# A one-core transformer block on Trainium2: the first weight unit cast in halves, two Gelus moved ahead of an exponential, an earlier residual, and a last root on ScalarE

## The reference

```
xn = rmsnorm(h, norm1_g);  p = xn @ w_in                     # 43 units of 128 columns
h  = h + mixer(p)                                            # attention, RWKV-7 recurrence, gates, w_proj, w_out
xn = rmsnorm(h, norm2_g);  q = xn @ peer_wq                  # 16 units
s  = q . subkeys;          top 16 of 128, twice; top 16 of the 256 sums   # per token and head
gates = softmax(best_s)
out[c] = sum over picked experts of  gelu(peer_u[e] . xn[c]) * gate[c, e] * peer_v[e]
return rmsnorm(h + out, normf_g)
```

## Time and profile before

| | |
|---|---|
| median of 3 runs | 1052.23 (1051.84 to 1052.33) |
| the profiled execution, its time | 1051.79 |
| its span in the trace | 1050.0 |
| TensorE busy | 1038.8 of the span |
| VectorE, ScalarE, GpSimd busy | 703.3, 640.2, 474.1 |
| granted TensorE clock, mean | 0.999 |
| data read from HBM | 179.37 MB, 172 GB/s over the span |

### The profile page before, as it was taken

How to read it: one execution, slowest core, us unless ns; L and a number is a source line. 1 busy time by engine, 2 the same in 40 slices (tenths; PEclk the granted TensorE clock), 3 DMA queues, 4 the chain that set the end, 5 groups by cost and what they waited for, 6 DMA issues and landing times.

```text
span 1050.0 us, 22101 instructions
## 1 busy us (share of the span) xinstructions
PE 1038.8 (99%) x6992; PEld 915.7 (87%) x6992; DVE 703.3 (67%) x1625; ACT 640.2 (61%) x1251; POOL 474.1 (45%) x228
## 2 busy tenths in 40 slices
PE   9999999999999999999999999999999999999997
PEld 8998899999998888888888888878888888888886
DVE  7765555445459999697888888855555555555554
ACT  7773475555566555657888888864544544544544
POOL 4685533884269888887777777730000000000000
PEclk9999999999999999999999999999999999999999
DMA  7463312556545555555444444455555555555554
GB/s 263 159 217 107 121 44 81 181 183 219 180 141 184 194 181 191 169 183 177 160 157 153 155 156 157 160 165 196 194 188 197 192 190 197 192 189 199 189 191 140
DMA packets 52136, 181.03 MB, mean 172 GB/s; under 512 B 5812, under 2 KB 7860, under 8 KB 51965
## 3 DMA queue, kind: packets, MB, share of 16 engines
q1 hardware_dynamic: 51660, 179.91, 51.2%
q10 hardware_dynamic: 432, 0.55, 0.2%
HBM read 179.37 MB, written 1.06 MB: 172 GB/s over the span
## 4 chain that ended last, share of the span: by engine, by line
PE 89%; DVE 9%; ACT 1%; DMA 0%; issue 0%; ACTq 0%; DVEq 0%
PE PS L436 19%; PE PS L888 11%; PE PS L889 11%; PE PS L887 11%; PE PS L440 10%; PE PS L426 6%; PE PS L427 5%; PE PS L428 5%; PE PS L838 2%; PE PS L839 1%; DVE PS L1429 1%; DVE PS L1808 1%; DVE PS L1812 1%; DVE con L1815 1%; PE PS L590 1%; DVE arena L1778 1%
## 5 line engine op out<-in xcount | busy, mean ns | idle before, releaser
L1324 POOL TENSOR_TENSOR lo<-raw,hi 128x1024 fp32r<-128x1024 f32 x191 | 463.4, 2432 | 191.8 <-ACT hi L934 179.7
L934 ACT CAST hi<-raw 128x1024 fp32r<-128x1024 f32 x331 | 346.5, 1047 | 193.0 <-DMA raw<-in_v_units 170.9
L436 PE MATMUL PS<-xb,hi 128*128 128x512 f32 x1088 | 279.3, 398 | 1.0 <-ACT arena L1209 1.0
L1383 DVE TENSOR_TENSOR lo<-raw,hi 128x1024 fp32r<-128x1024 f32 x140 | 171.6, 1226 | 157.4 <-ACT hi L934 157.4
L436 PEld LDWEIGHTS PS<-xb,hi 128*128 128x128 f32 x1088 | 194.9, 189 | 38.1 <-issue 2.4
L887 PE MATMUL PS<-hi,xb 128*128 128x512 f32 x512 | 199.3, 389 | 0.0
L889 PE MATMUL PS<-lo,xb 128*128 128x512 f32 x512 | 199.2, 389 | 0.0
L888 PE MATMUL PS<-hi,xb 128*128 128x512 f32 x512 | 199.2, 389 | 0.0
L440 PEld LDWEIGHTS PS<-xb,lo 128*128 128x128 f32 x1088 | 148.4, 190 | 11.0
L440 PE MATMUL PS<-xb,lo 128*128 128x256 f32 x1088 | 151.4, 282 | 0.0
L887 PEld LDWEIGHTS PS<-hi,xb 128*128 128x128 f32 x512 | 96.1, 188 | 20.1
(11 more groups left out here) (309 smaller groups left out, 1455.1 us busy)
## 6 DMA issues: line engine op xcount, KB each, us to landing
raw<-in_u_units SPq DMA_DIRECT2D x128, 512.0 KB, 3.3
raw<-in_v_units SPq DMA_DIRECT2D x128, 512.0 KB, 3.2
raw<-in_w_in_units SPq DMA_DIRECT2D x43, 512.0 KB, 3.3
raw<-in_w_q_units SPq DMA_DIRECT2D x16, 512.0 KB, 3.4
raw<-in_w_proj_units SPq DMA_DIRECT2D x8, 512.0 KB, 3.3
raw<-in_w_out_units SPq DMA_DIRECT2D x8, 512.0 KB, 4.3
arena<-bias_rows SPq DMA_DIRECT2D x2, 512.0 KB, 4.6
arena<-in_subkeys_t SPq DMA_DIRECT2D x1, 1024.0 KB, 6.5
```

The costliest lines, as they stand in the source:

```text
L436: mm(PS[:, bank, :], hi[:, s, P * k:P * k + P], both[:, k].rearrange("p s t -> p (s t)"), start=(k == 0), stop=False, skip_group_check=True)
L934: nc.scalar.copy(hi[:, j, :], raw[:, j, :]).then_inc(hi_made, 1)
L1324: nc.gpsimd.tensor_tensor(lo[:, w, :], raw[:, w, :], hi[:, w, :].bitcast(F32), ALU.subtract).then_inc(lo_pool, 1)
L1383: V.tensor_tensor(lo[:, w, :], raw[:, w, :], hi[:, w, :].bitcast(F32), ALU.subtract).then_inc(lo_dve, 1)
```

## The change

It has six parts.

1. ScalarE casts unit 0's high part in two halves, the first ahead of `uh` 6 and 7, with a count of its own (`hi_half`). Unit 1's cast moves ahead of the root of x. TensorE takes three of the four square sums, four slices of unit 0's high products, the last square sum, and the other four slices.
2. TensorE runs unit 1's high products ahead of unit 0's low ones. Units 3, 4 and 5 take their high products first and wait for the low part behind them. VectorE makes `ul` 2 and 3 ahead of its last square.
3. VectorE's ranking: one more `ranked` for each of the two index tables of a token tile, four in all, of 2 x 128 + 105 columns.
4. ScalarE: the Gelus of units 46 and 47 ahead of the exponential.
5. TensorE's wait for unit 127's Gelu ahead of the residual goes. What stays is the wait for the units that lie in banks 0 and 1, and for the gates in banks 2 and 3.
6. The last root: ScalarE adds the two sums inside the root (scale and bias of one activation), and VectorE inverts behind it.

```diff
@@ TensorE, start
-            for q in range(4):
+            def square_sums(q):
                 pe.wait_ge(sq_dve, q + 1)
                 for k in (2 * q, 2 * q + 1):
                     last = mm(PS[:, 7, 0:T], ones, sq[:, k, :], start=(k == 0), stop=(k == KT - 1))
-            last.then_inc(ss_ps, 1)
-            low_last(0)
-            low_last(1)
-            low_last(2)
+                return last
+            square_sums(0)
+            square_sums(1)
+            square_sums(2)
+            pe.wait_ge(hi_half, 1)
+            with_high(0, range(0, 4))
+            square_sums(3).then_inc(ss_ps, 1)
+            pe.wait_ge(hi_made, 1)
+            with_high(0, range(4, KT))
+            pe.wait_ge(hi_made, 2)
+            with_high(1)
+            pe.wait_ge(lo_dve, 1)
+            with_low(0)
+            pe.wait_ge(lo_pool, 2 - LO_FIRST)
+            with_low(1)
+            pe.wait_ge(hi_made, 3)
+            with_high(2)
+            pe.wait_ge(lo_pool, 3 - LO_FIRST)
+            with_low(2)
@@ in_unit
-                if g not in WIDE:
+                if g not in WIDE and g >= PLAIN_UNITS:
                     pe.wait_ge(lo_pool, g + 1 - LO_FIRST)
...
                 elif g < PLAIN_UNITS:
-                    product(PS[:, unit_bank(g), 0:T], g % 4, uh, ul).then_inc(unit_done, 1)
+                    with_high(g)
+                    pe.wait_ge(lo_pool, g + 1 - LO_FIRST)
+                    with_low(g)
@@ ahead of the residual
-            pe.wait_ge(act_evac, evacs + 2)
@@ ScalarE, start
             for q in range(4):
                 act.wait_ge(x_in[q], 16)
+                if q == 3:
+                    act.wait_ge(landed[0], 16)
+                    nc.scalar.copy(hi[:, 0, 0:D // 2], raw[:, 0, 0:D // 2]).then_inc(hi_half, 1)
...
-            make_hi(0, 0)
+            nc.scalar.copy(hi[:, 0, D // 2:D], raw[:, 0, D // 2:D]).then_inc(hi_made, 1)
+            make_hi(0, 1)
             act.wait_ge(ss_ps, 1)
...
-            for j in range(1, RAW):
+            for j in range(2, RAW):
                 make_hi(0, j)
@@ ScalarE, exponential
             hi_ahead(U_U, PICKS_AT, 0)
+            first_half_gelu(PICKS_AT, -2)
+            first_half_gelu(PICKS_AT, -1)
             act.wait_ge(shift_made, 2)
             nc.scalar.activation(bvs, bvs, ACT.Exp).then_inc(exp_made, 1)
@@ ScalarE, end
-            root(1)
-            act.wait_ge(fin_root, 2)
+            act.wait_ge(fin_sq, 4)
+            act.wait_ge(fin_inv, 2)
+            nc.scalar.activation(rms[:, 3:4], rms[:, 3:4], ACT.Sqrt, scale=1.0 / D, bias=rms[:, 2:3]).then_inc(fin_root, 1)
+            act.wait_ge(fin_done, 1)
@@ VectorE, start
             square_x(2)
+            split_low(2, 3)
             square_x(3)
-            split_low(2, 3, 4, 5, 6, 7)
+            split_low(4, 5, 6, 7)
@@ VectorE, ranking
                     link(V.tensor_copy(bpf, place))
+                    ranked(2 * P + RANK_FIXED)
                     for half in range(2):
@@ VectorE, end
             dve.wait_ge(fin_sq, 3)
+            V.tensor_scalar(rms[:, 2:3], rms[:, 2:3], 1.0 / D, RMS_EPS, ALU.mult, ALU.add).then_inc(fin_inv, 1)
             V.tensor_tensor(PS[:, 2, :], PS[:, 2, :], gain_all[:, 0:512], ALU.mult).then_inc(gained, 1)
-            link(V.tensor_scalar(rms[:, 2:3], rms[:, 2:3], D * RMS_EPS, None, ALU.add))
-            dve.wait_ge(fin_sq, 4)
-            link(V.tensor_scalar(rms[:, 3:4], rms[:, 3:4], rms[:, 2:3], 1.0 / D, ALU.add, ALU.mult))
-            V.reciprocal(rms[:, 3:4], rms[:, 3:4]).then_inc(fin_inv, 1)
             dve.wait_ge(fin_root, 2)
+            V.reciprocal(rms[:, 3:4], rms[:, 3:4]).then_inc(fin_done, 1)
+            dve.wait_ge(fin_done, 1)
```

More of the change, by code:

```diff
@@ L261, in block_program @@
         landed = [sem(f"unit_landed{j}") for j in range(RAW)]
-        hi_made = sem("hi_made")
+        hi_made, hi_half = sem("hi_made"), sem("first_half_of_first_unit_high")
         lo_dve = sem("lo_made_by_vector")
@@ L319, in block_program @@
         gained, gain_in, fin_act = sem("gain_applied"), sem("gain_in"), sem("fin_scaled_by_scalar")
+        fin_done = sem("last_inverse_root_made")
         fin_sq, fin_inv, fin_root, fin_sb, stored = (sem("fin_sq"), sem("fin_inverse"), sem("fin_root"),
@@ L472, in _, with with_high @@
                     last = mm(PS[:, 7, 0:T], ones, sq[:, k, :], start=(k == 0), stop=(k == KT - 1))
-            last.then_inc(ss_ps, 1)
-            def low_last(g):
-                pe.wait_ge(hi_made, g + 1)
-                for k in range(KT):
+                return last
+            def with_high(g, ks=range(KT)):
+                for k in ks:
                     c = slice(P * k, P * k + P)
@@ L482, in low_last, with with_low @@
                         pe.wait_ge(ul_made, k + 1)
[L483 to L488, removed]
+                    o = PS[:, unit_bank(g), 0:T]
+                    mm(o, hi[:, g % 4, c], uh[:, k, :], start=(k == 0), stop=False)
+                    mm(o, hi[:, g % 4, c], ul[:, k, :], start=False, stop=False)
+            def with_low(g):
                 for k in range(KT):
-                    last = mm(PS[:, g, 0:T], lo[:, g, P * k:P * k + P], uh[:, k, :], start=False, stop=(k == KT - 1))
+                    last = mm(PS[:, unit_bank(g), 0:T], lo[:, g % 4, P * k:P * k + P], uh[:, k, :], start=False, stop=(k == KT - 1))
                 last.then_inc(unit_done, 1)
-            low_last(0)
-            low_last(1)
-            low_last(2)
+            square_sums(0)
[16 more added lines that the diff above has]
+            with_low(2)
             def in_unit(g, tile_ready=None):
                 pe.wait_ge(hi_made, g + 1)
-                if g not in WIDE:
+                if g not in WIDE and g >= PLAIN_UNITS:
                     pe.wait_ge(lo_pool, g + 1 - LO_FIRST)
@@ L871, in _ @@
                     gated_unit(i, j)
-            evacs += NKEYS
-            pe.wait_ge(act_evac, evacs + 2)
             def residual(n):
@@ L1230, in _ @@
                 right_copy(PICKS_AT, j)
-                first_half_gelu(PICKS_AT, j - 2)
+                if j >= 2:
+                    first_half_gelu(PICKS_AT, j - 2)
             with act.Fori(PICKS_AT + 1, HALF // 4) as i:
@@ L1300, in squares @@
                                      accum_out=rms[:, b:b + 1]).then_inc(fin_sq, 1)
-            def root(n):
-                act.wait_ge(fin_inv, n + 1)
-                nc.scalar.activation(rms[:, 3 * n:3 * n + 1], rms[:, 3 * n:3 * n + 1], ACT.Sqrt).then_inc(fin_root, 1)
             squares(0)
             squares(1)
-            root(0)
+            act.wait_ge(fin_inv, 1)
+            nc.scalar.activation(rms[:, 0:1], rms[:, 0:1], ACT.Sqrt).then_inc(fin_root, 1)
             squares(2)
             squares(3)
-            root(1)
-            act.wait_ge(fin_root, 2)
+            act.wait_ge(fin_sq, 4)
+            act.wait_ge(fin_inv, 2)
+            nc.scalar.activation(rms[:, 3:4], rms[:, 3:4], ACT.Sqrt, scale=1.0 / D, bias=rms[:, 2:3]).then_inc(fin_root, 1)
+            act.wait_ge(fin_done, 1)
             act.wait_ge(gained, 1)
```

## The result

Forecast was 1047.7. The changed kernel took **1055.73** (median of 7 runs, 1054.19 to 1056.32), the kernel before 1052.33 on the same chip (7 runs): ratio 1.0028, 95% interval 1.0018 to 1.0038. It is slower by 3.4 in the medians, where 4.5 less was forecast. The profiled execution took 1054.50 for a span of 1052.7, at a granted clock of 0.999 in both kernels.

The account below looks back on a forecast made before the run. TensorE, busy 1038.8 of 1050.0, was taken as the bound, so only its waits could shrink. Gains 0.48 + 0.85 + 1.02 + 1.75 + 0.4 = 4.5 off 1052.23 gave 1047.7, range 1046.9 to 1049.2.

Parts of the forecast that it names:

- Start, 0.48: Start of the kernel: unit 1's low products begin at 14.7 for 15.18, 0.48 gained, bounds 0 to 0.6.
- The first rival (given back): LoRA products: slot 0's reload, late by 0.9 or more, gives the start's 0.48 back; 1048.2, chance 0.15.
- It just holds: LoRA products: due at 25.53, the low parts they want at worst 25.5, so the later reload costs nothing.
- Ranking and exponential, 1.87: Expert units 42 to 52: earlier ranking gains 0.85, two Gelus ahead of the exponential 1.02; together between 1.0 and 1.9.
- The picks are in no hurry: Behind the exponential: it ends at 437.8, VectorE needs some 1.6, and the picks are due only at 442.88.
- I take nothing off: Unit 51's low part could give back up to 0.9; not deducted, since the earlier ranking lets ScalarE reach the load earlier.
- unit 51's cast: Behind the exponential: this cast becomes the new wait, its low part up to 0.9 late; 1048.6, chance 0.12.
- The rival with idle time behind the table loads: ScalarE's exponential: each table load followed by idle time of its own length, unit 51 up to 3.4 late; 1050.5, chance 0.01.
- most of: ScalarE's exponential: with the Trainium skill's drain of 1.38 per load, most of the 1.87 would be lost at unit 51.
- Residual, 1.75: Between last gate matmul and `peer_v`: first product at 694.15 for 695.90, 1.75 gained, bounds 0.86 to 1.8.
- Last root, 0.4: End of the kernel: scaling at 1045.66 for 1046.07, 0.4 gained, bounds 0.3 to 0.5.

Follow-up runs that it names:

- the one with all in PSUM: Changed kernel with the picks' arithmetic in PSUM, and the ranking's additions, index conversion and copy of best scores with one PSUM operand: 1048.18, ratio 0.9963.

## Why the prediction was wrong

- **Start, 0.48: mis-sized, 0.1.** Unit 1's low products came at 13.92 + 0.96 = 14.88 for 14.7, the LoRA products at 25.71 for 25.53. Slot 0's reload was issued 1.6 later and not 0.9 (15.08 for 13.46), and the cast behind it began at 19.25 for 18.39. From there ScalarE ran 0.86 later: unit 5's cast at 24.81 for 23.95, and GpSimd's row of three low parts, units 5 to 7, at 25.92 for 25.07. Unit 6's low part, the second of the row, ended at about 30.64, and unit 6 (row below) started right behind it: 0.16 earlier than before, where the LoRA products had been 0.30 earlier. At expert unit 0 it was 0.09. The first rival (given back) had the mechanism and the wrong place: the step that failed was "It just holds", checked at the LoRA products and not one unit on.
- **Ranking and exponential, 1.87: right up to the transposes (1.97), and wrong behind them.** The step that failed is "The picks are in no hurry", with the "I take nothing off" of part 4. I asked only whether the picks are ready for the transposes, not what VectorE's arithmetic behind them meets; I priced the later casts at unit 51's low part alone, and took VectorE's durations as fixed. What the runs showed in its place: four short instructions held for GpSimd's row of low parts, 1.50 to 2.51 each, and a fifth behind them, which cost 5.7 up to the first gate matmul and nothing once the arithmetic was in PSUM (37.09 for 42.71). None of the rivals held this case. The nearest, unit 51's cast, did not come true: its low part ended at 441.48, ahead of its low products at 441.84. The rival with idle time behind the table loads (priced at 2.8, where the part on the exponential says "most of" 1.87) did not either: the load ends at 435.93, the exponential starts at 435.94.
- The Trainium skill states the rule, in "SBUF — State Buffer", section "Who interferes with whom": GpSimd shares a pair of SBUF ports with VectorE as an exclusive lock, taken by VectorE's copies and scalar operations from SBUF to SBUF and by those with two SBUF inputs, and whoever comes second waits out the other's whole instruction. The traces agree: those kinds were held up to 2.5, while the reciprocal and everything with a PSUM operand was not.
- The row that would have warned was in the trace of before: the cast L1840 took 2.38, its neighbours 0.42 and 0.43. A duration six times its neighbour's was a wait in disguise, and busy time counts it as work.
- **Residual, 1.75: right.** 1.65 in the traces, 1.8 in the medians of the run with this part alone. All sixteen transposes ran without a gap, as forecast.
- **Last root, 0.4: right**, 0.43.
- **`peer_v` loop, not forecast, 1.05.** Unit 127's low part ended at 1042.34 and TensorE stood for 0.8, until 1042.44. Its load took 4.3 from issue to landing, 3.2 in the trace of before. The same stall, within 0.1, stands in two other traces, of the experiment with parts 3 and 4 alone and of the one with all in PSUM, again with 4.2 to 4.4; in the other traces the last loads took 3.0 to 3.5 and no stall stands there. With one trace of each kernel it can't be said whether the kernel or the run decides, and the cause stays open. So does why four of the changed kernel's seven runs lie at 1055.73 to 1056.32 and three at 1054.19 to 1054.50; the profiled one is of the three.

The row of unit 6 in the trace after:

```profile
30.75 0.36 PE L427 MATMUL PS<-xb,hi 128*128 128x256 f32 x1
```

With the arithmetic in PSUM the forecast was near: 3.9 gained in the medians (1052.27 to 1048.36) of 4.5. The start's shortfall is 0.4 of what is missing.

## What to carry to other kernels

Before moving work earlier, look at what the engines around it have in hand at its new place: an engine that stops waiting also takes away the time in which another caught up. Compare the durations of equal shapes in the trace. If one is a multiple of the others, ask whether it holds a wait: here each such instruction ended with a low part of GpSimd. Short VectorE arithmetic beside a busy GpSimd belongs in PSUM when one operand is there already.

## What the runs showed that I had not expected

- A VectorE instruction of 0.3 to 0.43 took up to 2.51 behind one low part of GpSimd (2.41), and a 128x1024 sum of two SBUF operands 2.7 on average, with 1.22 the shortest of the four. The other way round the traces show little: the low part at 450.19 began inside VectorE's instruction of 450.15 and took 2.52, 0.1 more than those behind it.
- A copy of 128x256 fp32 from SBUF to SBUF took 0.28 when free, and the same copy from PSUM 0.42, so PSUM is the slower place when GpSimd is idle.
- Parts 3 and 4 each brought the transposes forward. Part 3 without part 4 was harmless (1049.16); part 4 without part 3 cost 5.7 behind them (1055.84).
